# VectorE writes the first chunk's high half behind two residuals, and the low pass takes two units side by side

## What is computed

```python
mix = concat([diff_attention, stick_breaking_attention]) @ w_o
x = x + rmsnorm(mix, attn_post_norm)          # residual 1 (touched)
h = rmsnorm(x, ffn_pre_norm)
u = causal_conv(h @ w_up); gate, val = split(u)
y = (gelu(gate) * val) @ w_down
x = x + rmsnorm(y, ffn_post_norm)             # residual 2 (touched)
h = rmsnorm(x, ffn1_norm)                     # second block
x = x + 0.5 * swiglu(h, ffn1_w_in, ffn1_w_out)
x = x + hybrid_mixer(rmsnorm(x, mix_norm))    # three kinds of attention
x = x + 0.5 * swiglu(rmsnorm(x, ffn2_norm), ffn2_w_in, ffn2_w_out)
return rmsnorm(x, final_norm)
```

## Time and profile before

| | us |
|---|---|
| runs shown (3) | 1652.4, 1652.62, 1652.94; median 1652.62 |
| the profiled execution's own time | 1652.4 |
| its span, first to last instruction | 1650.6 |
| TensorE busy | 1628.0 (99% of the span) |
| VectorE, ScalarE, GpSimd busy | 693.2, 672.8, 753.6 |
| mean granted TensorE clock | 0.998 of full |

### The profile page before, as it was taken

The page is one execution under the profiler, slowest core; times in us unless marked ns, Lnnn a source line. Parts: engine busy times, 40 slices in busy tenths (PEclk is TensorE's granted clock), DMA queues, the critical chain, the costliest instruction groups (busy, mean ns, idle before and its releaser), DMA issues.

```text
span 1650.6 us, 21039 instructions
## 1 busy us (share of the span) xinstructions
PE 1628.0 (99%) x8108; PEld 1351.2 (82%) x8108; DVE 693.2 (42%) x1399; ACT 672.8 (41%) x1181; POOL 753.6 (46%) x574
## 2 busy tenths in 40 slices
PE   9999999999999999999999999999999999999997
PEld 8788778888888888888888888888888888888886
DVE  7176756874444226311212225555773311112224
ACT  6355645543334234422222324567563422223322
POOL 7424334564444552744445552643114554445550
PEclk9999999999999999999999999999999999999999
DMA  5411102322223221322222222312002322222231
GB/s 204 147 52 52 52 1 102 115 96 96 102 89 103 94 98 56 123 92 101 101 90 102 89 102 90 103 65 78 27 27 90 102 90 102 91 101 99 93 102 51
DMA packets 42115, 147.35 MB, mean 89 GB/s; under 512 B 4768, under 2 KB 5152, under 8 KB 42016
## 3 DMA queue, kind: packets, MB, share of 16 engines
q1 hardware_dynamic: 40680, 143.39, 25.0%
q10 hardware_dynamic: 1336, 2.63, 0.5%
HBM read 142.84 MB, written 3.41 MB: 89 GB/s over the span
## 4 chain that ended last, share of the span: by engine, by line
PE 81%; DVE 3%; issue 1%; ACT 1%; POOL 1%; DMA 0%; DVEq 0%; ACTq 0%; POOLq 0%
PE PS L525 20%; PE PS L526 20%; PE PS L527 20%; PE PS L1099 5%; PE PS L494 4%; PE PS L1110 3%; PE PS L931 2%; PE PS L501 2%; PE PS L906 2%; PE PS L924 1%; POOL w_lo L569 0%; DVE L L1022 0%; DMA stage<-in_weights 0%; PE PS L547 0%; ACT sq L969 0%
## 5 line engine op out<-in xcount | busy, mean ns | idle before, releaser
L569 POOL TENSOR_TENSOR w_lo<-stage,w_hi 128x512 fp32r<-128x512 f32 x524 | 709.4, 1378 | 829.2 <-ACT w_hi L557 828.3
L557 ACT ACTIVATE w_hi<-stage 128x1024 fp32r<-128x1024 f32 x262 | 274.5, 1056 | 509.8 <-DMA stage<-in_weights 507.8
L525 PE MATMUL PS<-H_hi,w_hi 128*128 128x512 f32 x992 | 387.6, 391 | 0.4 <-DVE rcol L1288 0.4
L527 PE MATMUL PS<-H_hi,w_lo 128*128 128x512 f32 x992 | 386.0, 389 | 0.0
L526 PE MATMUL PS<-H_lo,w_hi 128*128 128x512 f32 x992 | 385.9, 389 | 0.0
L525 PEld LDWEIGHTS PS<-H_hi,w_hi 128*128 128x128 f32 x992 | 186.2, 188 | 40.4 <-issue 1.0
L526 PEld LDWEIGHTS PS<-H_lo,w_hi 128*128 128x128 f32 x992 | 186.2, 188 | 39.3 <-issue 1.0
L527 PEld LDWEIGHTS PS<-H_hi,w_lo 128*128 128x128 f32 x992 | 186.2, 188 | 38.6
L525 PE MATMUL PS<-A_hi,w_hi 128*128 128x512 f32 x528 | 205.6, 389 | 0.3 <-DVE A_lo L679 0.2
L694 DVE TENSOR_TENSOR conv<-PS,rstd 128x512 f32<-128x512 f32 x88 | 56.5, 686 | 354.7 <-PE PS L527 338.6
L526 PE MATMUL PS<-A_lo,w_hi 128*128 128x512 f32 x528 | 205.4, 389 | 0.0
(11 more groups left out here) (223 smaller groups left out, 2038.5 us busy)
## 6 DMA issues: line engine op xcount, KB each, us to landing
stage<-in_weights SPq DMA_DIRECT2D x262, 512.0 KB, 3.2
out_t<-Y SPq DMA_DIRECT2D x8, 256.0 KB, 2.0
X<-in_x_t SPq DMA_DIRECT2D x3, 512.0 KB, 8.5
bias_line<-bias_line ACTq DMA_DIRECT2D x1, 1270.0 KB
strip<-bias_line ACTq DMA_DIRECT2D x1, 1024.0 KB, 4.9
stage<-in_weights SPq DMA_DIRECT2D x2, 256.0 KB, 4.6
V<-QF SPq DMA_DIRECT2D x4, 128.0 KB, 2.3
V<-QF SPq DMA_DIRECT2D x4, 127.8 KB, 2.3
```

The source lines that it names most:

```text
L525: pe.matmul(out, a, h_hi, start=first, stop=False, skip_group_check=skip)
L527: return pe.matmul(out, b, h_hi, start=False, stop=last, skip_group_check=skip)
L557: act.activation(w_hi[:, slot, :], stage[:, slot, :], ACT.Copy).then_inc(hi_done, 1)
L569: lo = pool.tensor_tensor(w_lo[:, slot, cols], stage[:, slot, cols], w_hi[:, slot, cols].bitcast(F32), ALU.subtract)
```

## The change

Behind both touched residuals, and only there (a norm of kind "fold" that follows one of kind "post" is marked lead):

- In `dve_post`, VectorE first computes x_gained = X[0] * next gain with a tensor_scalar, into a free part of conv. For each half of chunk 0 it scales into `first` (also in conv), and then writes H_hi[0] = first * next gain + x_gained itself with a scalar_tensor_tensor, in place of the addition to X. ScalarE folds only chunks 1 to 7. TensorE waits for chunk 0's high half on the new semaphore lead_hi.
- The addition of `first` to X[0] stands last in `dve_post`, behind chunk 7, and VectorE waits for it before the folds. ScalarE waits for it before the squares.
- The low pass of `pe_first` takes units 0 and 1 side by side, then units 2 and 3: for each chunk two matmuls. Both units of a pair are reported done at the pair's end.
- `pe_warm` runs 12 matmuls in place of 14.

```diff
--- before.py
+++ after.py
@@ -363,6 +363,10 @@
                 if before is None and at > 1:
                     self.ready = sem(f"{name}_ready")
                 self.fold = kind == "fold"
+
+                self.lead = self.fold and before is not None
+                if self.lead:
+                    self.lead_hi, self.lead_done = sem(f"{name}_lead_hi"), sem(f"{name}_lead_done")
                 self.adds = KC - 1 if self.fold else KC - 3 if kind == "final" else KC - 2
                 self.banks = (2, 4) if kind == "final" else (STAT, 2)
 
@@ -380,14 +384,24 @@
                     self.scaled = sem(f"{name}_scaled")
                 if kind == "post":
                     self.x_done = sem(f"{name}_x_done")
+                    self.lead_in = sem(f"{name}_lead_in")
 
             def wait_ready(self, eng, k):
                 if self.at == 1:
                     eng.wait_ge(x_loaded[k // 2] if k else x0_loaded, 16)
                 elif self.before is None:
                     eng.wait_ge(self.ready, k + 1)
+                elif k == 0:
+                    eng.wait_ge(self.lead_done, 1)
                 else:
-                    eng.wait_ge(self.before.x_done, k + 1)
+                    eng.wait_ge(self.before.x_done, k)
+
+            def wait_hi(self, eng, k):
+
+                if self.lead and k == 0:
+                    eng.wait_ge(self.lead_hi, 1)
+                else:
+                    eng.wait_ge(self.hi, k + 1 - self.lead)
 
             def place(self, k):
 
@@ -463,13 +477,15 @@
 
         def act_norm(act, n):
 
+            if n.lead:
+                n.wait_ready(act, 0)
             for k in range(KC):
                 act_square(act, n, k, X[:, k, :])
             act_inverse(act, n)
 
         def dve_fold(dve, n, k):
 
-            dve.wait_ge(n.hi, k + 1)
+            n.wait_hi(dve, k)
             c = n.order[k]
             dve.scalar_tensor_tensor(out=H_lo[:, c, :], in0=X[:, c, :], scalar=pc(n.name, c),
                                      in1=H_hi[:, c, :].bitcast(F32), op0=ALU.mult,
@@ -487,37 +503,45 @@
             for part in ([range(units - late), range(units - late, units)] if late else [range(units)]):
                 pe.wait_ge(lo_done, u0 + part[-1] + 1)
                 for k in range(KC):
-                    pe.wait_ge(n.hi, k + 1)
+                    n.wait_hi(pe, k)
                     c = n.order[k]
                     for j in part:
                         for w in (w_hi, w_lo):
                             pe.matmul(PS[:, j, :], w[:, (u0 + j) % RING, bass.ts(c, P)], H_hi[:, c, :],
                                       start=(k == 0 and w is w_hi), stop=False)
-            for j in range(units):
+            for js in ([[0, 1], [2, 3]] if n.lead else [[j] for j in range(units)]):
                 for k in range(KC):
-                    if j == 0:
+                    if js[0] == 0:
                         pe.wait_ge(n.done, k + 1)
                     c = n.order[k]
-                    m = pe.matmul(PS[:, j, :], w_hi[:, (u0 + j) % RING, bass.ts(c, P)], H_lo[:, c, :],
-                                  start=False, stop=(k == KC - 1))
-                m.then_inc(unit_done, 1)
-
-        def dve_post(dve, n):
-
+                    for j in js:
+                        m = pe.matmul(PS[:, j, :], w_hi[:, (u0 + j) % RING, bass.ts(c, P)], H_lo[:, c, :],
+                                      start=False, stop=(k == KC - 1))
+                        if k == KC - 1:
+                            m.then_inc(unit_done, 1)
+
+        def dve_post(dve, n, following):
+
+            x_gained, first = conv[:, 1, 0, :], conv[:, 1, 1, :]
+            dve.tensor_scalar(x_gained, X[:, 0, :], pc(following.name, 0), None, ALU.mult).then_inc(n.lead_in, 1)
+            dve.wait_ge(n.lead_in, 1)
             for half, cols in enumerate(halves()):
                 dve.wait_ge(norm_inverse, n.passed - 1 + half)
-                dve.scalar_tensor_tensor(out=tmp[:, 0, cols], in0=n.place(0)[:, cols], scalar=pc(n.name, 0),
+                dve.scalar_tensor_tensor(out=first[:, cols], in0=n.place(0)[:, cols], scalar=pc(n.name, 0),
                                          in1=rstd[:, cols], op0=ALU.mult, op1=ALU.mult).then_inc(n.scaled, 1)
                 dve.wait_ge(n.scaled, half + 1)
-                add = dve.tensor_tensor(X[:, 0, cols], X[:, 0, cols], tmp[:, 0, cols], ALU.add)
-            add.then_inc(n.x_done, 1)
+                lead = dve.scalar_tensor_tensor(out=H_hi[:, 0, cols], in0=first[:, cols], scalar=pc(following.name, 0),
+                                                in1=x_gained[:, cols], op0=ALU.mult, op1=ALU.add)
+            lead.then_inc(following.lead_hi, 1)
             for k in range(1, KC):
-                if k >= 2:
-                    dve.wait_ge(n.x_done, k - 1)
+                if k >= 3:
+                    dve.wait_ge(n.x_done, k - 2)
                 dve.scalar_tensor_tensor(out=tmp[:, k % 2, :], in0=n.place(k), scalar=pc(n.name, k),
                                          in1=rstd[:, :], op0=ALU.mult, op1=ALU.mult).then_inc(n.scaled, 1)
                 dve.wait_ge(n.scaled, k + 2)
                 dve.tensor_tensor(X[:, k, :], X[:, k, :], tmp[:, k % 2, :], ALU.add).then_inc(n.x_done, 1)
+            dve.tensor_tensor(X[:, 0, :], X[:, 0, :], first, ALU.add).then_inc(following.lead_done, 1)
+            dve.wait_ge(following.lead_done, 1)
 
         def split_matmul(pe, out, w_slot, w_cols, h_hi, h_lo, first, last, skip=False):
 
@@ -1715,7 +1739,7 @@
                 for u in WO_NEXT.get(at, ()):
                     act_next(act, U_WO + u)
             act_inverse(act, n_attn_post)
-            for k in range(KC):
+            for k in range(1, KC):
                 act_fold(act, n_ffn_pre, k)
             act_next(act, U_WO + KC - 1)
             act_norm(act, n_ffn_pre)
@@ -1830,11 +1854,11 @@
             pe_wo_rest(pe, 0, at1)
             pe.wait_ge(n_attn_post.ready, KC - 1)
             pe_stat(pe, n_attn_post)
-            pe_warm(pe, 14)
+            pe_warm(pe, 12)
             pe_ffn(pe, 0, U_UP1, U_DN1, n_ffn_pre)
             pe.wait_ge(y_moved, len(MOVED))
             pe_stat(pe, n_ffn_post)
-            pe_warm(pe, 14)
+            pe_warm(pe, 12)
             pe_ffn(pe, 1, U_UP2, U_DN2, n_ffn1)
             pe_first(pe, n_mix, U_MIX, 4)
             pe_stat(pe, n_mix)
@@ -1906,7 +1930,7 @@
             dve_turn1(dve, 0, 7)
             for k in range(1, n_attn_post.adds + 1):
                 dve_add(dve, n_attn_post, k)
-            dve_post(dve, n_attn_post)
+            dve_post(dve, n_attn_post, n_ffn_pre)
             for k in range(KC):
                 dve_fold(dve, n_ffn_pre, k)
             dve_norm(dve, n_ffn_pre)
@@ -1914,7 +1938,7 @@
             for k in range(1, n_ffn_post.adds + 1):
                 dve_add(dve, n_ffn_post, k)
             dve.wait_ge(y_moved, len(MOVED))
-            dve_post(dve, n_ffn_post)
+            dve_post(dve, n_ffn_post, n_ffn1)
             for k in range(KC):
                 dve_fold(dve, n_ffn1, k)
             dve_norm(dve, n_ffn1)
```

## The result

The changed kernel is slower: a median of 1655.26 us over 19 runs (1654.73 to 1659.03), against 1652.70 us over 19 runs of the kernel before (1652.21 to 1656.57). That is 2.56 us; the ratio is 1.0016 with an interval of 1.0009 to 1.0022. The profiled executions took 1655.07 and 1652.4, their spans are 1653.3 and 1650.6. Single executions of either kernel lie up to 4 us above their median, so this interval reaches about 1 us to each side, and those of the experiments 1.5 us; the medians are steadier (the kernel before gave 1652.70, 1652.72, 1652.80, 1652.87 and 1652.49 in five sets).

The account below looks back on a forecast made before the run. The prediction took VectorE's chain to the sum-of-squares matmul as the bound: 0.79 + 0.79 for the residuals + 0.12 for x_gained = +1.7 us, median 1654.3; own range 1653.4 to 1654.9, 8 in 10 1652.3 to 1656.0.

Parts of the forecast that it names:

- What bounds: At the sum-of-squares matmul (line 431) TensorE's and VectorE's chains meet; VectorE's is already later, by 0.18 us.
- The lead: Chunk 0 on VectorE: scalar_tensor_tensor takes 0.48 us against the addition's 0.42, twice, so +0.12.
- The last addition: Addition for chunk 0, now in front of VectorE's folds and waited for: +0.73 us per residual.
- The bound without a wait: Lower bound for the addition placed before the folds, if VectorE did not wait for it: 0.61 us.
- The folds and GpSimd: VectorE's folds begin 0.85 us later; two pass, two are held by GpSimd, four follow; additions +0.79.
- x_gained: Hidden in residual 2; in residual 1 contention with GpSimd costs 0 to +0.24 us, taken as +0.12.
- TensorE's chain: High pass starts 0.64 us earlier, waits 0.32 for chunk 1; low pass unheld; then 1.46 wait before the sum.
- Sum: 0.79 for each of two residuals plus 0.12 for x_gained: +1.7 us.
- nothing later takes it up: Behind the two residuals the delay stays whole, since TensorE's other waits are tenths of a us in 1650.
- the gain in front: Rival: the sum is in time and TensorE's chain sets the end, -0.67 us per residual, 1651.3; 7%.
- the folds met GpSimd twice: Forecast: two held folds of 1.78 us remain; rivals had one hit (1652.2, 8%) or hits one earlier (1655.6, 9%).
- a fall: Rival: granted clock drops from 2.4 to 1.2 GHz at TensorE's wait before the sum, 2.7 us each, 1659.7; 3%.

Follow-up runs that it names:

- e1: Kernel before, with only the low pass changed, units side by side behind both residuals: 1652.54 us against 1652.72 (ratio 0.9997).
- e2: Changed kernel with the low pass put back to unit after unit: 1654.91 us against 1652.72 of the kernel before (1.0010).
- e6: Kernel before, with the low pass side by side and more buffers for the squares: 1651.53 us against 1652.80 (0.9990).
- e5: Kernel before, with more buffers for the squares behind the two residuals: 1651.85 us against 1652.80 (0.9996).
- e3: Changed kernel with the last addition to X[0] done on 8 of 512 tokens only: 1653.95 us against 1652.72 of the kernel before (1.0006).
- e4: Kernel before, with four extra matmuls of ones in front of the sum's matmul behind both residuals: 1653.74 us against 1652.72 (1.0002).
- e7: Changed kernel with more buffers for the squares: 1653.68 us against 1652.80 of the kernel before (1.0005).
- e10: Changed kernel with more buffers for the squares and the last addition to X[0] moved to GpSimd: 1654.22 us against 1652.87 of the kernel before (1.0010).

## Why the prediction came out as it did

The forecast was 1654.3, +1.7. The measured 1655.26 is 2.56 over the kernel before; it lies within the range for 8 in 10 (1652.3 to 1656.0) and 0.4 above the forecast's own (1653.4 to 1654.9). The mechanism was right, and the two changed places came out as added up; what the sum left out lies elsewhere. Step by step:

- *What bounds.* Right, and the point on which all hangs: VectorE's chain to line 431 was already the later one. e1, e2 and e6 show it from three sides.
- *The lead.* Predicted 0.48 long, and it is 0.48; the chunk takes 1.83 (640.59 to 642.42) where 1.84 was said.
- *The last addition.* Predicted 0.73, measured 0.72. The bound without a wait, 0.61, is ruled out. The waited-for addition takes 0.72 to the next start, the others 0.61 (651.53 to 652.14). The others raise a semaphore too, so it is the wait that costs 0.11. The rule cited from the Trainium skill ("VectorE: DVE Perf Modes", section "The DRAIN you can't avoid"), that a semaphore after each instruction costs nothing extra, was measured there on a row of copies; for these additions it does not hold if the semaphore is waited for.
- *The folds and GpSimd.* Two pass, two are held, four follow, as said. I had them absorb 0.06 of the shift, and they absorbed little: 0.84 and 0.83 in place of 0.79.
- *x_gained.* It took 1.51 in residual 1 beside GpSimd, against 0.48 in residual 2, so its kind contends with GpSimd as well. But the first scaling was held to 1.02, as before, and the sum is 0.84 later here and 0.83 behind residual 2. The 0.12 I gave it is 0.
- *TensorE's chain.* Behind residual 1 the high pass starts 2.61 after the first scaling (272.56 to 275.17) in place of 3.24; 0.64 was predicted, 0.63 came. It then waits in front of chunk 1, but less than the 0.32 said: behind residual 2 the eight matmuls on chunk 0 take 2.06 to the next one (642.65 to 644.71). I had reckoned them at 1.82, and in the kernel before, where nothing holds chunk 1, they take 1.93 (641.76 to 643.69, and not 643.59 as I had it), so 0.13 of it is wait. The low pass has no wait; the wait in front of the sum is 1.36 and 1.38, where 1.46 was said.
- *Sum.* 1.67 at the two places, 1.70 predicted. The step that failed is "nothing later takes it up, as TensorE's other waits are tenths of a us": they are tenths, but not constants. One of them grew by 0.35, since another instruction had come to the number in VectorE's stream that is late. The remaining 0.5 of the 2.56 has no certain cause. In the profiled execution it is the clock at 209 us and the start of the program, neither of which is the change's doing by anything shown here. The 0.12 too much for x_gained and the 0.09 too little for the folds nearly cancelled, which was luck.

Of the rivals, the gain in front did not arrive, and the folds met GpSimd twice as before. The clock held its level at the new waits: granted 1.00 in all of 297 to 301 and 665 to 669 us. But my evidence against a fall, the idle of 2.3 us in front of a transpose that had left the clock at 1.00, came from a single execution, and the last section shows that it was a matter of luck.

## What to carry to other kernels

Where two chains meet at one instruction, the later one is the price of both: before an edit that hastens the earlier one by a hop, add up what it puts on the later one. A piece of work that is moved to the end of its engine's list so as to be out of the way is still in the way of whatever that engine does next for the bottleneck. And when the wait of the engine that bounds the kernel just changes its name (here from H_lo to the sum and back), the cure lies with the engine it waits for: more buffers for the squares brought what the reordering could not.

## What the runs showed of the hardware beyond that

**The granted clock at a 2.33 us idle is not the same each time.** In front of the transposes at 209 us TensorE is idle for 2.33 us in the traces of all 14 kernels. In the kernel before the clock stayed at 1.00. In the changed kernel's profiled execution, at this place ahead of any changed code:

```profile
207.00:209.00 2.00, 0.17 (x2) 0.00 (x0) 1.97 (x5) 1.94 (x5) 0.00 (x0) 1.00 0.01 4
209.00:211.00 2.00, 1.50 (x9) 1.54 (x9) 1.97 (x3) 1.10 (x5) 1.32 (x2) 0.69 0.00 0
211.00:213.00 2.00, 2.00 (x8) 1.56 (x8) 1.69 (x5) 1.74 (x3) 1.00 (x1) 0.50 0.00 0
```

These are the busy times by stretch, as in the earlier trace rows; the third column from the right is the clock. It fell from 2.4 to 1.2 GHz right behind the idle. In e5's profiled execution it stayed down longer:

```profile
213.00:217.00 4.00, 4.00 (x18) 3.11 (x18) 3.09 (x5) 0.60 (x2) 0.00 (x0) 0.50 0.00 0
217.00:221.00 4.00, 4.00 (x18) 3.55 (x16) 1.31 (x4) 1.15 (x3) 0.00 (x0) 0.50 0.00 0
```

That execution took 1655.8 where e5's median is 1651.85. Set beside the kernel before's matmul by matmul, the trace of e5 loses 3.9 us between 206 and 225 us, that of e3 1.6 and that of the changed kernel 0.25. The clock fell there in seven of the 14 profiled executions (the changed kernel, e2, e3, e4, e5, e7, e10), with and without the lead, and not in the other seven. So it is one source of the executions that lie some 4 us over their median. In the kernel before, which was profiled only without the fall, such executions have a lower mean clock as well: beside e1, 0.995 in the four from 1655.86 to 1656.91, and 0.998 or 0.999 in the 20 shortest. The waits of 1.4 us in front of the sum, with dense matmuls around them, show no fall in any of the profiled executions.

**A wait costs TensorE a bit more than its length:** from the sum's matmul to the next one's start it is 0.56 where the sum's matmul had to wait and 0.46 where it had not (in e4, and in e6 663.16 to 663.62).

**Small instructions that nothing needs can move a wait** by some tenths of a us through VectorE's stream, over 500 us behind where they stand: four memsets took the wait at the transpose from 0.8 to 0.5, seven in the other kernel took it from 0.4 to 0.6. A difference of so much between two builds says nothing of an edit before the trace has placed it.
